# A two-layer decoder trunk on one core: input and output projections cut at the prompt's end instead of in the middle

## The chip, the core and the metric

The kernel runs on one NeuronCore of a Trainium2 chip. The engines named below are TensorE (PE, matrix products, with its weight loads on a row of their own, PEld), VectorE (DVE), ScalarE (ACT), GpSimd (POOL) and SyncE (SP, which issues the transfers). The metric is the device time of one launch in microseconds (us).

## What is computed

The reference is a decoder trunk of two layers, applied to a prompt of 512 tokens and to 8 samples of 8 tokens (64 tokens), with the same weights. Cut to what matters:

```python
def mixer_layer(x, ...states..., norm_w, w_in, ..., w_out):
    h = rmsnorm(x, norm_w)
    proj = jnp.einsum('bld,de->ble', h, w_in)          # 1024 -> 5648 columns
    z, xbc, dt_raw, q, k, v, g_ret, u, g_pool = split_cols(proj, IN_SIZES)
    ...                                                # causal conv, SSD scan -> y_ssd (1024)
    ...                                                # rotary, retention     -> y_ret (512)
    ...                                                # windowed means        -> y_pool (512)
    mix = jnp.concatenate([y_ssd, y_ret, y_pool], axis=-1)
    x = x + jnp.einsum('ble,ed->bld', mix, w_out)      # 2048 -> 1024
    return x, new_states
```

All inputs and outputs are f32. The two `einsum` with `w_in` and `w_out`, over 576 tokens, are the projections this document is about.

## The kernel before

**Layout.** Channels lie on the 128 partitions and the 576 tokens (`TOK`: 512 of the prompt, then 64 of the samples, `SMP`) along the free axis. A projection is cut into units of 128 output channels: unit `u` multiplies a weight block of 8 x 128 x 128 (`KT` = 8 chunks `k` of the contraction) with 576 token columns. A layer has 61 units (`UNITS`): 0 to 44 make the branches' inputs (dt, q, k, v, conv, pool, gates, z), 45 to 52 (`U_OUT` on) are the output projection from `mix`, and 53 to 60 the one from the SSD output in `hin`. Both layers run the same loop body.

**Precision.** Each operand is split into a high part in the type fp32r and a low part, the rest. ACT makes the high part of a weight block (`high`, L799), DVE subtracts it to get the low part (`split`, L1029). `products` (L493 to L500) then makes three matmuls for each `k` and each half of the tokens: high weights x high tokens, high weights x low tokens, low weights x high tokens. A half is 288 columns (`HALF`), and each half has a PSUM bank of its own: `acc_of(u)` is `acc[:, u % 2, :, 0:288]`, two banks for even and two for odd units. So a unit is 2 x 8 x 3 = 48 matmuls of 288 columns. Each matmul has its own weight load in the trace, also where the next one uses the same weights.

**Order.** Each engine runs an order written out by hand, unit by unit ("slots"). PE runs `project(u)`: wait until the weights are split (`w_split`) and until the accumulator of unit u-2 has been read (`evac`, or `x_new` for output units), then the first half over all `k`, then a piece of branch work (`between`), then the second half; after it further branch work may stand (`ssd_turn`, `ssd_y`, `ret_turn`, `pool_mm_`, `ssd_sums`). At the end of a unit PE raises `proj`. ACT then makes the next-but-one weights' high part and reads the accumulator out (`read_out`). DVE's slot `u` runs `before(u)` first, which holds work that PE's `between` of the same unit has made ready (`pool_gate`, `ret_sample_y`, `ret_add`, `ssd_add`), then `split(u + 2)`, which waits for ACT, and then the branch's vector work.

**The stretch of the sample states.** In units 37 to 41 (`S_SST` = 37) the SSD states of the samples (`h0`, eight tiles named h in the trace) are renewed. PE makes four groups of sums (`ssd_sums(q, g)`, L619): (0,0) in the middle of unit 39, (0,1) after unit 39, (1,0) in the middle of unit 40, (1,1) after unit 40. Each but the first waits for DVE to have added the sums before it (`ssd_add`, L1232, semaphore `hs_n`). DVE's order there is: slot 39 begins with `ssd_add(0,0)`, `ssd_decayed` (L1222), `ssd_add(0,1)`; slot 40 begins with `ssd_add(1,0)`, slot 41 with `ssd_add(1,1)`. PE's norm sums after unit 41 wait for the fourth add. `pool_gate(i)` (L1379) reads what `pool_mm_(i)` (L725) has put into the accumulator of unit 33+i, and PE waits for it before it projects unit 35+i into the same banks.

Of the kernel before, what the change touches and what calls it, by code (L numbers as in the profile page):

```python
# [20 lines left out]
HALF = TOK // 2  # L21
KT = D_MODEL // P
# [106 lines left out]
def trunk(nc: bass.Bass, a):  # L129
    with ExitStack() as ctx:  # L130
# [13 lines left out]
        def sem(name):  # L144
# [15 lines left out]
              for i, o in enumerate((2048, 3072, 4096, 5120, 0, 1024, 6144, 8192))]  # L160
# [52 lines left out]
               stk[0:SMP, 0:RP * P], ssq[0:SMP, 0:RP * P]]  # L213
        ones_ = place("ones", [P, P])
# [11 lines left out]
        def acc_of(u):  # L226
            return acc[:, u % 2, :, 0:HALF]

# [27 lines left out]
        evac = sem("acc_read")  # L256
        x_new = sem("x_updated")
# [228 lines left out]
        def _(pe):  # L486
# [6 lines left out]
            def products(u, half, k):  # L493

                out = acc_of(u)[:, half, :]
                hi, lo = operands(u, k, slice(half * HALF, (half + 1) * HALF))
                wh, wl = w_hi[:, u % 2, k, :], w_lo[:, u % 2, k, :]
                pe.matmul(out, wh, hi, start=k == 0, stop=False)  # L498
                pe.matmul(out, wh, lo, start=False, stop=False)  # L499
                return pe.matmul(out, wl, hi, start=False, stop=k == KT - 1)  # L500

            def project_first():

                for step in range(KT + LAG):
                    for u, k in ((0, step), (1, step - LAG)):
# [4 lines left out]
                        for half in range(2):  # L510
                            mm = products(u, half, k)
# [3 lines left out]
            def project(u, between=None):  # L515
# [7 lines left out]
                for half in range(2):  # L523
                    for k in range(KT):
                        if half == 0 and o == 0:
                            pe.wait_ge(mix_lo, k + 1)
                        if half == 0 and o == OUT_CHUNKS:
                            pe.wait_ge(y_lo, k + 1)
                        mm = products(u, half, k)
                    if half == 0 and between is not None:  # L530
                        between()
# [187 lines left out]
            def pool_mm_(g):  # L719

                pe.wait_ge(pooled_ok, g + 1)
                pe.wait_ge(evac, U_GPOOL + g + 1)
                dst = acc_of(U_GPOOL + g)
                for half in range(2):
                    mm = pe.matmul(dst[:, half, :], pw[:, g, :], halves(vT[:, g, :])[:, half, :],  # L725
                                   start=True, stop=True)
                mm.then_inc(pool_mm, 1)
# [64 lines left out]
        def _(eng):  # L792
# [26 lines left out]
            def read_out(u):  # L819

                src = acc_of(u)
                if u == U_DT:
                    go(act(halves(dt_raw), src[0:HEADS], ACT.Identity, bias=hvec[:, 0:1]), evac, u + 1)
                elif u < U_V:
# [4 lines left out]
                    go(act(halves(qk[:, i, :]), src, ACT.Copy, scale=1.0 if i < RP else HD ** -0.5), evac, u + 1)  # L829
                elif u < U_CONV:  # L830
                    go(act(halves(vT[:, u - U_V, :]), src, ACT.Copy), evac, u + 1)
                elif u < U_GRET:
# [4 lines left out]
                    go(act(hb[:, w:w + HALF], src[:, 0, :], ACT.Copy))  # L837
                    go(act(hb[:, w + HALF:w + SEQ], src[:, 1, 0:SEQ - HALF], ACT.Copy))
                    go(act(hb[:, w + SEQ:].rearrange("p (b n) -> p b n", b=NB)[:, :, w:],
                           src[:, 1, SEQ - HALF:].rearrange("p (b n) -> p b n", b=NB), ACT.Copy), evac, u + 1)  # L840
                elif u < U_GPOOL:
                    go(act(halves(qk[:, RP + u - U_GRET, :]), src, ACT.Silu), evac, u + 1)
                elif u < U_Z:
# [3 lines left out]
                    go(act(halves(tmp[:, i % 2, :]), src, ACT.Silu), evac, u + 1)  # L847
                else:
# [5 lines left out]
                    go(act(halves(z_gate[i % 4]), src, ACT.Silu), evac, u + 1)  # L854
# [67 lines left out]
            with eng.Fori(0, DEPTH) as l:  # L922
# [4 lines left out]
                for u in range(UNITS):  # L927
# [21 lines left out]
                    if u < U_OUT:  # L949
                        read_out(u)  # L950
# [13 lines left out]
                    if U_CONV < u <= U_POOL:  # L964
# [770 lines left out]
```

## Time and profile before

| | us |
|---|---|
| median of 3 runs | 1001.88 |
| lowest, highest | 1001.37, 1003.04 |
| the profiled execution | 999.01 |
| its span, first to last instruction | 997.3 |
| PE busy | 946.2 (95%) |
| weight loads busy | 903.7 |
| DVE busy | 675.4 (68%) |
| ACT busy | 436.5 (44%) |

The profiled execution took 999.01 us, of which 1.7 us lie outside its span. A matmul's duration in the trace includes its way through the array, so consecutive matmuls overlap in the timeline: what one matmul costs is read from the distance between the starts of neighbours, not from its duration. A plain f32 matmul stands in the trace as two records, each with a weight load; an fp32r matmul and a transpose stand as one.

### The profile page before, as it was taken

How to read it: one execution, taken by the hardware profiler on the slowest of the kernel's cores; microseconds unless marked ns; L12 is line 12 of the kernel's file. 1: busy time of each engine (PE TensorE's matmuls, PEld its weight loads, DVE VectorE, ACT ScalarE, POOL GpSimd, SP SyncE). 2: the span in 40 equal slices, each digit the busy share in tenths (PEclk: the TensorE clock that was granted, in tenths of full speed). 3: DMA queues.
4: the chain of work that ended last, by engine and by line, in shares of the span. 5: the costliest groups of instructions: out<-in, count | busy, mean ns of one | idle time of the engine just before them, and what ended most of it. 6: DMA issues, size and time to landing. Idle time of an engine off the chain costs nothing.

```text
span 997.3 us, 19050 instructions
## 1 busy us (share of the span) xinstructions
PE 946.2 (95%) x7930; PEld 903.7 (91%) x7930; DVE 675.4 (68%) x912; ACT 436.5 (44%) x707; POOL 44.5 (4%) x148
## 2 busy tenths in 40 slices
PE   1999999999999989999869999999999999999994
PEld 1999999999989779999869999999989987999993
DVE  5796478876895559654459927777679758576444
ACT  5423355334884246522443325532367633644222
POOL 0000011110010000000000001110101000000000
PEclk9999999999999999999979999998999999999997
DMA  6625222234234363322144522221433451552223
GB/s 264 206 71 146 79 64 65 70 100 156 85 103 161 137 231 129 116 85 85 45 156 152 147 86 64 65 64 49 149 107 100 142 199 46 225 184 85 79 55 134
DMA packets 36825, 116.82 MB, mean 117 GB/s; under 512 B 11168, under 2 KB 11808, under 8 KB 35072
## 3 DMA queue, kind: packets, MB, share of 16 engines
q1 hardware_dynamic: 36480, 114.68, 34.6%
q8 instruction: 64, 1.05, 0.4%
q0 software_dynamic: 256, 0.88, 0.3%
q14 instruction: 25, 0.20, 0.1%
HBM read 95.72 MB, written 19.83 MB: 116 GB/s over the span
## 4 chain that ended last, share of the span: by engine, by line
PE 89%; DVE 5%; ACT 2%; DMA 1%; issue 1%; POOLq 0%; DVEq 0%; SPq 0%; ACTq 0%
PE acc L498 26%; PE acc L500 25%; PE acc L499 25%; PE misc L582 2%; DVE h L1232 1%; PE misc L568 1%; PE misc L585 1%; PE misc L635 1%; DVE w_lo L1029 1%; DVE h L1222 1%; PE misc L554 1%; PE misc L676 1%; PE misc L657 1%; PE acc L725 1%; PE misc L599 1%
## 5 line engine op out<-in xcount | busy, mean ns | idle before, releaser
L498 PE MATMUL acc<-hin,w_hi 128*128 128x288 f32 x1696 | 510.3, 301 | 16.8 <-DVE hin L1425 16.7
L499 PE MATMUL acc<-hin,w_hi 128*128 128x288 f32 x1696 | 502.1, 296 | 0.0
L500 PE MATMUL acc<-hin,w_lo 128*128 128x288 f32 x1696 | 502.0, 296 | 0.0
L498 PEld LDWEIGHTS acc<-hin,w_hi 128*128 128x128 f32 x1696 | 320.8, 189 | 31.2 <-DVE hin L1425 18.0
L799 ACT ACTIVATE w_hi<-w_raw 128x1024 fp32r<-128x1024 f32 x122 | 129.1, 1058 | 450.9 <-PE acc L500 439.9
L499 PEld LDWEIGHTS acc<-hin,w_hi 128*128 128x128 f32 x1696 | 321.0, 189 | 0.3
L500 PEld LDWEIGHTS acc<-hin,w_lo 128*128 128x128 f32 x1696 | 320.7, 189 | 0.0
L1029 DVE TENSOR_TENSOR w_lo<-w_raw,w_hi 128x1024 fp32r<-128x1024 f32 x124 | 151.3, 1220 | 197.4 <-ACT w_hi L799 197.3
L498 PE MATMUL acc<-mix,w_hi 128*128 128x288 f32 x256 | 76.2, 298 | 0.0
L500 PE MATMUL acc<-mix,w_lo 128*128 128x288 f32 x256 | 75.5, 295 | 0.0
L499 PE MATMUL acc<-mix,w_hi 128*128 128x288 f32 x256 | 75.4, 294 | 0.0
L1099 DVE SCALAR_TENSOR_TENSOR conv_out<-halo,vec,conv_out 128x600 f32<-128x600 f32 x72 | 60.8, 844 | 2.5
L884 ACT ACTIVATE decay<-decay,token_vecs 128x128 f32<-128x128 f32 (+1 forms) x160 | 47.8, 379 | 1.4
L499 PEld LDWEIGHTS acc<-mix,w_hi 128*128 128x128 f32 x256 | 48.0, 188 | 0.2
L498 PEld LDWEIGHTS acc<-mix,w_hi 128*128 128x128 f32 x256 | 48.0, 188 | 0.2
L500 PEld LDWEIGHTS acc<-mix,w_lo 128*128 128x128 f32 x256 | 48.0, 188 | 0.0
L807 ACT ACTIVATE tmp<-x 128x576 f32<-128x576 f32 x24 | 16.3, 683 | 31.2 <-DVE x L1441 30.1
L582 PE MATMUL misc<-decay,xdt 128*64 128x128 f32 (+1 forms) x320 | 27.3, 266 | 0.0
L1441 DVE TENSOR_TENSOR x<-x,acc 128x576 f32<-128x576 f32 x32 | 24.1, 754 | 3.7 <-PE acc L500 0.2
L582 PEld LDWEIGHTS misc<-decay,xdt 128*64 128x64 f32 (+1 forms) x320 | 19.4, 136 | 6.8 <-issue 6.8
L1146 DVE TENSOR_TENSOR xdt<-misc,token_vecs 128x1024 f32<-128x1024 f32 x10 | 12.2, 1225 | 19.6 <-PE misc L559 19.4
L1158 DVE TENSOR_TENSOR decay<-decay,scores 128x1024 f32<-128x1024 f32 (+1 forms) x20 | 21.5, 1113 | 2.4 <-ACT decay L891 1.7
(204 smaller groups left out, 1017.5 us busy)
## 6 DMA issues: line engine op xcount, KB each, us to landing
w_raw<-in_w SPq DMA_DIRECT2D x124, 512.0 KB, 3.7
decay<-cum_rows SPq DMA_DIRECT2D x8, 1024.0 KB, 6.0
h<-in_ssm SPq DMA_DIRECT2D x16, 512.0 KB, 6.2
out_ssm_s<-h SPq DMA_DIRECT2D x16, 512.0 KB, 6.8
x_kept<-x SPq DMA_DIRECT2D x2, 2304.0 KB, 8.5
x<-x_kept SPq DMA_DIRECT2D x8, 576.0 KB, 5.8
x<-in_x SPq DMA_DIRECT2D x4, 576.0 KB, 5.9
out_y<-x SPq DMA_DIRECT2D x4, 576.0 KB, 2.9
```

The lines of the kernel that those rows point to most:

```text
L498: pe.matmul(out, wh, hi, start=k == 0, stop=False)
L499: pe.matmul(out, wh, lo, start=False, stop=False)
L500: return pe.matmul(out, wl, hi, start=False, stop=k == KT - 1)
L582: mm = pe.matmul(dst[r, :], xdt[0:n, h * HD:(h + 1) * HD], decay[0:n, t % 2, h, 0:n], start=True, stop=not inter)
L799: go(act(w_hi[:, u % 2, :, :], w_raw[:, u % RAW, :, :], ACT.Copy), w_hid, n)
L807: go(act(tmp[:, j % 2, :], x[:, j, :], ACT.Square), sqd, j + 1)
L884: go(act(m, m, ACT.Relu, scale=-1.0, bias=tokv[0:n, t, h:h + 1]))
L1029: go(V.tensor_tensor(w_lo[:, u % 2, :, :], w_raw[:, u % RAW, :, :], w_hi[:, u % 2, :, :].bitcast(F32), ALU.subtract), w_split, n)
L1099: ins = V.scalar_tensor_tensor(out=o, in0=h[:, c:c + CVO], scalar=w[c], in1=o, op0=ALU.mult, op1=ALU.add)
L1146: go(V.tensor_tensor(heads(xdt[:, :]), src, dt_b, ALU.mult))
L1158: ins = V.tensor_tensor(m, m, gm[0:n, g, 0:n].unsqueeze(1).to_broadcast([n, 8, n]), ALU.mult)
L1441: go(V.tensor_tensor(halves(x[:, m, :]), halves(x[:, m, :]), acc_of(u), ALU.add), x_new, o + 1)
```

## The change

The projections are cut at column 512, the prompt's end, and not in the middle. For each `k` there are now five matmuls in place of six: three of 512 columns for the prompt, one of 128 columns in which the samples' high and low parts (64 columns each) stand side by side under the high weights, and one of 64 columns, low weights x high tokens, for the samples. All 1728 columns per `k` are there as before. The low parts' product therefore lands in columns of its own (64 to 127 of the second bank), together with the low weights' product, and has to be added to the first 64: for units up to 44 DVE does it at the start of its slot with a copy out of PSUM and an add in PSUM (`fold`, new semaphore `folded`, for which ACT's `read_out` waits); for the output units DVE adds it to `x` with one more instruction. `k` is now the outer loop and `between` stands after the fourth `k`. ACT reads the accumulator as one row of 576 (the convolution's halo in two pieces, not three). The pool's matmul is cut at 512 too.

```diff
+LEFT = SEQ
...
+        low = xbc_two[:, 10, TOK:]
...
         def acc_of(u):
-            return acc[:, u % 2, :, 0:HALF]
+            return acc[:, u % 2, :, :].rearrange("p a n -> p (a n)")[:, 512 - LEFT:512 - LEFT + TOK]
...
-            def products(u, half, k):
-
-                out = acc_of(u)[:, half, :]
-                hi, lo = operands(u, k, slice(half * HALF, (half + 1) * HALF))
+            def products(u, k):
+                out = acc_of(u)
+                a, b = slice(0, LEFT), slice(LEFT, TOK)
+                m = mix[:, k // 4, :, k % 4, :] if U_OUT <= u < U_OUT + OUT_CHUNKS else hin[:, :, k, :]
                 wh, wl = w_hi[:, u % 2, k, :], w_lo[:, u % 2, k, :]
-                pe.matmul(out, wh, hi, start=k == 0, stop=False)
-                pe.matmul(out, wh, lo, start=False, stop=False)
-                return pe.matmul(out, wl, hi, start=False, stop=k == KT - 1)
+                first, last = k == 0, k == KT - 1
+                both = acc[:, u % 2, 1, 0:2 * SMP].rearrange("p (a n) -> p a n", a=2)
+                pe.matmul(out[:, a], wh, m[:, 0, a], start=first, stop=False)
+                pe.matmul(out[:, a], wh, m[:, 1, a], start=False, stop=False)
+                pe.matmul(both, wh, m[:, :, b], start=first, stop=False)
+                pe.matmul(both[:, 1, :], wl, m[:, 0, b], start=False, stop=last)
+                return pe.matmul(out[:, a], wl, m[:, 0, a], start=False, stop=last)
...
-                for half in range(2):
-                    for k in range(KT):
...
-                        mm = products(u, half, k)
-                    if half == 0 and between is not None:
+                for k in range(KT):
...
+                    mm = products(u, k)
+                    if k == KT // 2 - 1 and between is not None:
                         between()
...
-                for half in range(2):
-                    mm = pe.matmul(dst[:, half, :], pw[:, g, :], halves(vT[:, g, :])[:, half, :],
-                                   start=True, stop=True)
+                for c in (slice(0, LEFT), slice(LEFT, TOK)):
+                    mm = pe.matmul(dst[:, c], pw[:, g, :], vT[:, g, c], start=True, stop=True)
...
-                    go(act(hb[:, w:w + HALF], src[:, 0, :], ACT.Copy))
-                    go(act(hb[:, w + HALF:w + SEQ], src[:, 1, 0:SEQ - HALF], ACT.Copy))
+                    go(act(hb[:, w:w + SEQ], src[:, 0:SEQ], ACT.Copy))
...
                     if u < U_OUT:
+                        wait(folded, u + 1)
                         read_out(u)
...
+            def fold(u):
+
+                wait(proj, u + 1)
+                two = acc[:, u % 2, 1, 0:2 * SMP].rearrange("p (a n) -> p a n", a=2)
+                settle()
+                go(V.tensor_copy(low, two[:, 1, :]))
+                settle()
+                go(V.tensor_tensor(two[:, 0, :], two[:, 0, :], low, ALU.add), folded, u + 1)
...
                 for u in range(UNITS):
+                    if u < U_OUT:
+                        fold(u)
                     before(u)
...
-                        go(V.tensor_tensor(halves(x[:, m, :]), halves(x[:, m, :]), acc_of(u), ALU.add),
+                        go(V.tensor_tensor(x[:, m, :], x[:, m, :], acc_of(u), ALU.add))
+                        settle()
+                        go(V.tensor_tensor(x[:, m, SEQ:], x[:, m, SEQ:], acc[:, u % 2, 1, SMP:2 * SMP], ALU.add),
                            x_new, o + 1)
```

`low` is a column range that no other work uses: the SSD's copy of the samples in chunks 10 and 11 of `xbc_two` is no longer written.

On PE, the middle of unit 39. Before, the last `k` of the first half, the sums, and the first two `k` of the second half:

```order
L498 MATMUL acc<-hin,w_hi 128x288
L499 MATMUL acc<-hin,w_hi 128x288
L500 MATMUL acc<-hin,w_lo 128x288
L619 MATMUL misc<-xdt_to_end,b_tok_seq 128x512 x4
L498 MATMUL acc<-hin,w_hi 128x288
L499 MATMUL acc<-hin,w_hi 128x288
L500 MATMUL acc<-hin,w_lo 128x288
L498 MATMUL acc<-hin,w_hi 128x288
L499 MATMUL acc<-hin,w_hi 128x288
L500 MATMUL acc<-hin,w_lo 128x288
```

After, the fourth `k`, the sums, and the fifth:

```order
L503 MATMUL acc<-hin,w_hi 128x512
L504 MATMUL acc<-hin,w_hi 128x512
L505 MATMUL acc<-hin,w_hi 128x128
L506 MATMUL acc<-hin,w_lo 128x64
L507 MATMUL acc<-hin,w_lo 128x512
L624 MATMUL misc<-xdt_to_end,b_tok_seq 128x512 x4
L503 MATMUL acc<-hin,w_hi 128x512
L504 MATMUL acc<-hin,w_hi 128x512
L505 MATMUL acc<-hin,w_hi 128x128
L506 MATMUL acc<-hin,w_lo 128x64
L507 MATMUL acc<-hin,w_lo 128x512
```

The sums stand at the same place, half-way through the unit; two short matmuls stand between the long ones, and the one with the low weights is followed by another with the same weights.

On DVE, the end of slot 39 and slot 40, h being the sample states. Before:

```order
L1029 TENSOR_TENSOR w_lo<-w_raw,w_hi 128x1024
L1222 TENSOR_TENSOR h_6_65<-h_6_65,exp_last_sample 128x1024
L1222 TENSOR_TENSOR h_7_66<-h_7_66,exp_last_sample 128x1024
L1232 TENSOR_TENSOR h_4_63<-h_4_63,misc 128x512
L1232 TENSOR_TENSOR h_5_64<-h_5_64,misc 128x512
L1232 TENSOR_TENSOR h_6_65<-h_6_65,misc 128x512
L1232 TENSOR_TENSOR h_7_66<-h_7_66,misc 128x512
L1029 TENSOR_TENSOR w_lo<-w_raw,w_hi 128x1024
```

After:

```order
L1037 TENSOR_TENSOR w_lo<-w_raw,w_hi 128x1024
L1239 TENSOR_TENSOR h_6_65<-h_6_65,exp_last_sample 128x1024
L1239 TENSOR_TENSOR h_7_66<-h_7_66,exp_last_sample 128x1024
L1054 COPY xbc<-acc 128x64
L1056 TENSOR_TENSOR acc<-acc,xbc 128x64
L1249 TENSOR_TENSOR h_4_63<-h_4_63,misc 128x512
L1249 TENSOR_TENSOR h_5_64<-h_5_64,misc 128x512
L1249 TENSOR_TENSOR h_6_65<-h_6_65,misc 128x512
L1249 TENSOR_TENSOR h_7_66<-h_7_66,misc 128x512
L1037 TENSOR_TENSOR w_lo<-w_raw,w_hi 128x1024
```

The fold now heads the slot, in front of the state adds for which PE waits, and it waits itself for the end of the unit's projection.

## Rows read from the trace of the kernel before

**Rows 1.** The page: busy us of the engines, and the chain that ended last.

```profile
PE 946.2 (95%) x7930; PEld 903.7 (91%) x7930; DVE 675.4 (68%) x912; ACT 436.5 (44%) x707; POOL 44.5 (4%) x148
...
PE 89%; DVE 5%; ACT 2%; DMA 1%; issue 1%; POOLq 0%; DVEq 0%; SPq 0%; ACTq 0%
PE acc L498 26%; PE acc L500 25%; PE acc L499 25%; PE misc L582 2%; DVE h L1232 1%; PE misc L568 1%; PE misc L585 1%; PE misc L635 1%; DVE w_lo L1029 1%; DVE h L1222 1%; PE misc L554 1%; PE misc L676 1%; PE misc L657 1%; PE acc L725 1%; PE misc L599 1%
```

**Rows 2.** Page, costliest groups: shapes, count | busy us, mean ns | idle before.

```profile
L498 PE MATMUL acc<-hin,w_hi 128*128 128x288 f32 x1696 | 510.3, 301 | 16.8 <-DVE hin L1425 16.7
...
L499 PEld LDWEIGHTS acc<-hin,w_hi 128*128 128x128 f32 x1696 | 321.0, 189 | 0.3
```

**Rows 3.** Timeline of PE, 450 to 458 us: start, duration, engine, line, operands.

```profile
450.06 0.29 PE L498 MATMUL acc<-hin,w_hi 128*128 128x288 f32 x1
450.19 0.30 PE L499 MATMUL acc<-hin,w_hi 128*128 128x288 f32 x1
450.33 0.29 PE L500 MATMUL acc<-hin,w_lo 128*128 128x288 f32 x1
...
457.61 0.29 PE L498 MATMUL acc<-hin,w_hi 128*128 128x288 f32 x1
```

**Rows 4.** Timeline of PE at the start of layer two.

```profile
507.39 0.45 PE L498 MATMUL acc<-hin,w_hi 128*128 128x288 f32 x1
507.63 0.45 PE L499 MATMUL acc<-hin,w_hi 128*128 128x288 f32 x1
```

**Rows 5.** Table of stretches: from:to, length, busy of PE, PEld, DVE, ACT, POOL, clock, DMA.

```profile
504.00:508.00 4.00, 1.49 (x6) 1.49 (x7) 3.85 (x6) 2.05 (x3) 0.00 (x0) 0.50 1.05 378
...
446.00:458.00 12.00, 12.00 (x92) 12.00 (x91) 3.80 (x5) 2.80 (x3) 0.00 (x0) 1.00 0.27 89
```

**Rows 6.** Timeline of PEld where PE had waited for weights.

```profile
521.78 0.19 PEld L498 LDWEIGHTS acc<-hin,w_hi 128*128 128x128 f32 x1 [0.29 <-DVE w_lo L1029]
521.89 0.19 PEld L499 LDWEIGHTS acc<-hin,w_hi 128*128 128x128 f32 x1
522.02 0.19 PEld L500 LDWEIGHTS acc<-hin,w_lo 128*128 128x128 f32 x1
```

**Rows 7.** The chain in order of time: start, length, what, how many.

```profile
114.77 1.09 PE misc L635 x16
...
238.63 1.72 PE misc L568 x4
...
306.42 0.97 PE acc L725 x4
```

**Rows 8.** Timeline of PE, 230 to 233 us, merged.

```profile
231.45 0.61 PE L556 MATMUL misc<-xbc 128*128 128x128 f32 x4
231.89 0.38 PE L559 MATMUL misc<-tab,xbc 128*128 128x128 f32 x2
```

**Rows 9.** Timeline of DVE, units 37 to 41 of layer one.

```profile
324.99 0.82 DVE L1379 SCALAR_TENSOR_TENSOR vT<-acc,vec,tmp 128x576 f32<-128x576 f32 x1 [1.21 <-PE acc L725]
...
343.91 2.48 DVE L1232 TENSOR_TENSOR h<-h,misc 128x512 f32<-128x512 f32 x4 [1.34 <-PE misc L619]
346.52 2.36 DVE L1222 TENSOR_TENSOR h<-h,exp_last_sample 128x1024 f32<-128x1024 f32 x2
...
358.94 2.48 DVE L1232 TENSOR_TENSOR h<-h,misc 128x512 f32<-128x512 f32 x4
...
367.89 1.62 DVE L1401 TENSOR_TENSOR xbc<-xbc,halo 128x576 f32<-128x576 f32 x2
```

**Rows 10.** Timeline of PE at the fourth state sums, layer one.

```profile
357.73 1.14 PE L619 MATMUL misc<-xdt_to_end,b_tok_seq 32*128 32x512 f32 x8 [1.57 <-DVE h L1232]
```

**Rows 11.** Groups by shape on DVE, whole run.

```profile
L1200 DVE SCALAR_TENSOR_TENSOR xbc<-xbc,vec,misc 128x64 f32<-128x64 f32 x16 | 3.2, 272 | 0.0
```

**Rows 12.** Waits: who for whom, us in total, times, longest.

```profile
ACT w_hi L799 <- PE acc L500: 439.9, 112, 11.6
...
PE misc L706 <- ACT rstd L899: 2.0, 2, 1.0
```

More of the change, by code:

```diff
@@ L256, in trunk @@
         evac = sem("acc_read")
+        folded = sem("sample_parts_folded")
         x_new = sem("x_updated")
@@ L522, in project @@
                     pe.wait_ge(x_new, o - 1)
-                for half in range(2):
-                    for k in range(KT):
[L525 to L529, printed above, removed]
-                    if half == 0 and between is not None:
+                for k in range(KT):
+                    if o == 0:
+                        pe.wait_ge(mix_lo, k + 1)
+                    if o == OUT_CHUNKS:
+                        pe.wait_ge(y_lo, k + 1)
+                    mm = products(u, k)
+                    if k == KT // 2 - 1 and between is not None:
                         between()
@@ L822, in read_out @@
                 if u == U_DT:
-                    go(act(halves(dt_raw), src[0:HEADS], ACT.Identity, bias=hvec[:, 0:1]), evac, u + 1)
+                    go(act(dt_raw, src[0:HEADS], ACT.Identity, bias=hvec[:, 0:1]), evac, u + 1)
                 elif u < U_V:
@@ L828, in read_out @@
                         wait(h_lo, KT)
-                    go(act(halves(qk[:, i, :]), src, ACT.Copy, scale=1.0 if i < RP else HD ** -0.5), evac, u + 1)
+                    go(act(qk[:, i, :], src, ACT.Copy, scale=1.0 if i < RP else HD ** -0.5), evac, u + 1)
                 elif u < U_CONV:
-                    go(act(halves(vT[:, u - U_V, :]), src, ACT.Copy), evac, u + 1)
+                    go(act(vT[:, u - U_V, :], src, ACT.Copy), evac, u + 1)
                 elif u < U_GRET:
@@ L846, in read_out @@
                         wait(pool_out, i - 1)
-                    go(act(halves(tmp[:, i % 2, :]), src, ACT.Silu), evac, u + 1)
+                    go(act(tmp[:, i % 2, :], src, ACT.Silu), evac, u + 1)
                 else:
@@ L853, in read_out @@
                         wait(g_z_used, i - 3)
-                    go(act(halves(z_gate[i % 4]), src, ACT.Silu), evac, u + 1)
+                    go(act(z_gate[i % 4], src, ACT.Silu), evac, u + 1)
             def ssd_row_exps(t):
@@ L970, in _ @@
                         sampled = cvt[:, i % 2, 3 + SEQ:HALO].rearrange("p (b n) -> p b n", b=NB)[:, :, 0:NT]
-                        go(act(xbc_two[:, k, SEQ:].rearrange("p (a b n) -> p a b n", a=2, b=NB),
-                               sampled.unsqueeze(1).to_broadcast([P, 2, NB, NT]), ACT.Silu, bias=cb),
-                           xbc_ok, i + 1)
+                        if k < 10:
+                            go(act(xbc_two[:, k, SEQ:].rearrange("p (a b n) -> p a b n", a=2, b=NB),
+                                   sampled.unsqueeze(1).to_broadcast([P, 2, NB, NT]), ACT.Silu, bias=cb),
+                               xbc_ok, i + 1)
+                        else:
+                            go(act(xbc[:, k, SEQ:].rearrange("p (b n) -> p b n", b=NB), sampled, ACT.Silu, bias=cb),
+                               xbc_ok, i + 1)
                     if S_RET <= u < S_RST and (u - S_RET) % 2 == 0:
@@ L1378, in pool_gate @@
                 settle()
-                go(V.scalar_tensor_tensor(out=halves(vT[:, i, :]), in0=acc_of(U_GPOOL + i), scalar=v_(V_PS + i),
-                                          in1=halves(tmp[:, i % 2, :]), op0=ALU.mult, op1=ALU.mult),
+                go(V.scalar_tensor_tensor(out=vT[:, i, :], in0=acc_of(U_GPOOL + i), scalar=v_(V_PS + i),
+                                          in1=tmp[:, i % 2, :], op0=ALU.mult, op1=ALU.mult),
                    pool_out, i + 1)
```

5 lines of the change are left out of this document (2 added, 3 removed).

## The prediction

> **What bounds the kernel now.** I read the page's busy times and its chain first [rows 1]. PE is busy for 95% of the span, 89% of the chain that ended last lies on it, and about 76% on the three lines of `products` alone. DVE is busy for 68%, and ACT spends 440 us waiting for PE to end a unit [rows 12]. So the kernel lasts as long as PE's string of projection matmuls, and a change of that string counts nearly in full. Next comes the question what one of these matmuls costs. The mean of 301 ns in the page [rows 2] is no answer, since neighbours overlap. In the timeline [rows 3] 57 matmuls lie between the starts at 450.06 and 457.61, which is 132.5 ns each, at a granted clock of 1.00 [rows 5], the 2.4 GHz level. There 288 columns need 120 ns, so 12.5 ns are something else. A unit is 48 x 132.5 = 6.4 us, and both layers have 2 x 61 x 8 = 976 steps of `k`, each now 6 x 132.5 = 795 ns.
>
> **What the 12.5 ns are.** Two rows tell. Where the granted clock was 0.50 (1.2 GHz) the spacing was 240 ns [rows 4, 5], exactly 288 columns, with nothing added. And the row of the weight loads [rows 6] shows that a load starts when the matmul before it starts: one load runs ahead, not more. After a wait, with no matmul running, load (521.78) to next load (521.89) is 110 ns; beside a running fp32r matmul it is 130 ns. So I read the spacing as that of the load: 110 ns alone, up to 133 ns beside a stream. Plain f32 records bear out the 110: a record of 128 columns with a full 128 x 128 load stands at (231.89 - 231.45) / 4 = 110 ns [rows 8]. The other reading is a fixed 12.5 ns on each matmul; it costs nearly the same below.
>
> **The projections after the change.** The columns per `k` stay 1728; what changes is what hides the loads. Three matmuls have 512 columns. Plain records of 512 columns stand at 1.72 / 4 = 430 ns [rows 7], at two cycles a column 427 ns, so 3 ns over. At one cycle a column that is 213 + 3 = 217 ns; with a fixed 12.5 ns it would be 226 ns. The two short ones need 53 and 27 ns for their columns, but each must last as long as the load of the matmul behind it: the load for the low weights starts with the 128-column matmul, and the load behind the 64-column one starts with that, though it fetches the same weights again (the same holds before: L499 loads what L498 had, once for each of its 1696 matmuls [rows 2]). That is 110 to 133 ns each. I take the middle, 121.5, since a short stream disturbs the load for only part of it. Sum per `k`: 3 x 217 + 2 x 121.5 = 894 ns, against 795. That is 99 ns x 976 = **96.6 us more**. Bounds: 651 + 220 = 871 ns (+74 us) and 3 x 226 + 266 = 944 ns (+145 us).
>
> **The fold.** Ninety times DVE now copies 128 x 64 out of PSUM and adds it back. The nearest row is 128 x 64 with PSUM as a source, 0.20 us each in a row, 272 ns alone [rows 11]; two that depend on each other make about 0.5 us (0.4 to 0.6). In an ordinary slot this costs nothing: it runs while ACT makes the next high part, for which DVE's `split` waits anyway, and unit and slot both have 6.4 us or more. The order matters more. `fold(u)` waits for the end of unit `u` and now stands in front of `before(u)`, which until now ran in the middle of the unit. I go through the places where PE waits for what `before` does:
> - Slot 37: `pool_gate(3)` began at 324.99 in mid-unit [rows 9]. Now it follows the fold, and PE needs it for unit 38: 0.5 + 0.8 + 0.1 = 1.4 us idle.
> - Slot 39: `ssd_add(0,0)` ran at 343.91, 2.5 us [rows 9]; PE's sums behind unit 39 need it. Now 0.5 + 2.5 + 0.1 = 3.1 us idle.
> - Slot 40: `ssd_add(1,0)` likewise 3.1 us, less the 1.6 us that PE waited for it already [rows 10]: 1.5 us.
> - Slot 41: `ssd_add(1,1)` (358.94) is needed by the norm sums behind unit 41: 3.1 us, of which about 1.1 us comes back, since PE waited there later for ACT, 1.0 us [rows 12], behind DVE's gates at 367.89 [rows 9]. 2.0 us.
>
> The other such places (`ret_add`, `ret_sample_y`, `pool_gate` 0 to 2) have half a unit or a piece of branch work between them and PE's need. Sum 8.0 us a layer, **16 us**; bounds 8 us, if PE finds part of it idle anyway, and 24 us.
>
> **The rest.** The pool's matmul: two records of 288 columns at 0.97 / 4 = 243 ns twice over [rows 7] become two of 430 and two of at least 110, 1.08 in place of 0.97 us, 8 times: **0.9 us**. The output units' additional DVE add is 0.25 us, hidden except at each layer's end; with the short matmuls at the 0.50 clock of a layer's start that makes **2 us** (0 to 4). ACT's merged halo reads save time on an engine that waits 440 us: nothing. The semaphore `folded` holds up ACT's read-out, but only PE's unit u+2 waits for that, a whole unit later: nothing.
>
> **Sum.** 96.6 + 16 + 0.9 + 2 = 115.5 us on the profiled execution's own 999.0 us (span 997.3 and 1.7 around it): 1114.5. The median of the runs lies 2.9 us above that execution: 1117.
>
> **Rivals.**
> A. *Short fp32r matmuls lose their single pass.* No row has one under 288 columns. If they ran like plain f32, the 128-column one would cost two records, 220 ns [rows 8], and the 64-column one 110 to 220. Sum 981 to 1091 ns, +182 to +289 us; I take 1000 ns, +200 us, with the rest 1222. For it: the trace says nothing of such sizes. Against it: type and operands are the same as at 288.
> B. *Loads do not bind, the other side.* If each short matmul costs its columns and 3 ns, 57 + 30, the sum is 651 + 87 = 738 ns, 56 us less, and with the 19 us of fold and rest the time is 965. With fixed 12.5 ns it is 784 ns and 1010. It would take loads that run two ahead. For it: in pairs of row groups with 64 x 128 weights records stand at 1.09 / 16 = 68 ns [rows 7]. Against it: those lie in different rows of the array, ours use all 128, and rows 6 and 8 show 110. The turning point: the change pays from 19 us / 976 = 20 ns less per `k`, so from a short pair below 124 ns, 62 each.
> The Trainium skill ("TensorE: Matmul & The Clock Gate", "Back-to-back issue gap") gives for a lone matmul N / 2.4 + 2.5 ns, by which the five would make 733 ns, case B.
> C. *Long matmuls cost less than their columns*, at the 132.5 ns of rows 3 also with 512: 3 x 132.5 + 2 x 110 = 618 ns, 173 us less, 848 in all. Against it stand the 430 ns of rows 7, which are all columns, and the 240 ns of rows 4.
> The same section of the Trainium skill states 131 ns for pairs of load and matmul at 512 columns and 81 at 128, which would make 555 ns; the trace disagrees with it at 512.
> D. *DVE falls behind.* If the fold's 0.5 us reached PE in all 90 slots, 45 us would come in place of none: 1162. Against it: DVE's 68% would fall to about 64% of the longer span.
>
> **How the numbers follow.** The forecast's own case 0.66, from 1085 to 1178 by its bounds; A 0.15, B 0.11, C 0.02, D 0.06. The likeliest gives 1117. The range takes in D and most of A: 1080 to 1225. Faster by over 0.2% (about what a measurement here can tell from no change) is C and most of B, 0.10; within it 0.01; slower 0.89.
>
> **What would show it.** In the new timeline: 512-column matmuls 217 ns apart (226: the fixed cost); from the 128-column start to the 64-column start and on to the next 110 to 133 ns each; 53 and 27 would be B, 213 and 107 or doubled records A. A unit of about 7.15 us. New waits of PE's L624 sums and of the norm sums for DVE, 3 us long, and of unit 38 for `pool_gate`, four a layer. Folds of 0.5 us, with ACT's wait for PE still in the hundreds of us. It is wrong from the root if the distance between matmuls is not what sets a unit's length.

## The result: 1141.6 us, 14% slower

| | before | after |
|---|---|---|
| median of the runs, us | 1002.0 | 1141.6 |
| lowest to highest | 1001.4 to 1003.0 | 1140.7 to 1143.4 |
| ratio, 95% interval | | 1.140 (1.138 to 1.143) |
| the profiled execution | 999.0 | 1142.0 |
| its span | 997.3 | 1140.3 |

The change costs 140 us where I had forecast 115 (1117 us, range 1080 to 1225). The direction and what bounds the kernel were right; two terms of the sum were too small, the matmuls of 512 columns and the stretch of the state adds. The page of the kernel after, the lines that answer to [rows 1] and [rows 2]:

```profile
PE 1072.0 (94%) x6954; PEld 898.1 (79%) x6954; DVE 723.3 (63%) x1124; ACT 435.5 (38%) x675; POOL 51.0 (4%) x148
...
PE 94%; DVE 3%; ACT 1%; issue 1%; DMA 0%; POOLq 0%; DVEq 0%; ACTq 0%
PE acc L507 27%; PE acc L503 21%; PE acc L504 20%; PE acc L506 7%; PE acc L505 5%; PE misc L587 2%; DVE h L1249 1%; PE misc L573 1%; PE misc L624 1%; PE misc L590 1%; PE misc L640 1%; PE misc L711 1%; PE misc L559 1%; PE misc L662 1%; PE acc L730 1%; PE misc L681 1%
...
L507 PE MATMUL acc<-hin,w_lo 128*128 128x512 f32 x848 | 409.9, 483 | 0.0
L503 PE MATMUL acc<-hin,w_hi 128*128 128x512 f32 x848 | 345.4, 407 | 20.0 <-DVE hin L1442 17.0
...
L506 PE MATMUL acc<-hin,w_lo 128*128 128x64 f32 x848 | 211.0, 249 | 0.0
...
L505 PE MATMUL acc<-hin,w_hi 128*128 128x128 f32 x848 | 188.1, 222 | 0.0
```

PE is as busy as before and more of the chain lies on it (94%). The two short matmuls, L505 and L506, are in the chain with 5% and 7% and have 11% of the columns together, but neither this share nor a duration is their cost: L506, 64 columns, lasts 249 ns in the trace and L505, 128 columns, 222. One record of L506 starts at 520.90 us, while the load of its weights started at 520.85 and takes 0.19 us, so its time is counted from before its weights are there.

The cost is read from the weight loads instead, since a load starts when the matmul before it starts [rows 6]. The timeline of PEld, start and duration in us, in the middle of a unit:

```profile
520.39 0.19 PEld L504 LDWEIGHTS acc<-hin,w_hi 128*128 128x128 f32 x1
520.62 0.19 PEld L505 LDWEIGHTS acc<-hin,w_hi 128*128 128x128 f32 x1
520.85 0.19 PEld L506 LDWEIGHTS acc<-hin,w_lo 128*128 128x128 f32 x1
520.95 0.19 PEld L507 LDWEIGHTS acc<-hin,w_lo 128*128 128x128 f32 x1
521.07 0.19 PEld L503 LDWEIGHTS acc<-hin,w_hi 128*128 128x128 f32 x1
521.30 0.19 PEld L504 LDWEIGHTS acc<-hin,w_hi 128*128 128x128 f32 x1
```

From the start at 520.39 on, the matmuls stand at 0.23, 0.23, 0.10, 0.12 and 0.23 us: three long ones of 231 ns and two short ones of 110 ns, in sum 914 ns per `k` where [rows 3] gave 795. A unit without branch work takes 7.305 us, before 6.36.

The waits of PE behind other engines, with us in total, number and longest. In the kernel before, the lines that answer to the first two waited 3.2 us (L619, for DVE) and 2.0 us (L706, for ACT) in all [rows 10, 12]:

```profile
PE misc L624 <- DVE h L1249: 12.7, 4, 3.2
PE misc L711 <- DVE h L1249: 6.5, 2, 3.3
PE acc L503 <- DVE vT L1396: 3.0, 2, 1.5
```

So the sum of the forecast stands against the two profiled executions like this:

| term, us | forecast | measured |
|---|---|---|
| projections | 96.6 | 0.945 a unit x 122 units = 115.3 |
| units 37 to 42 beyond that | 16 | 13.7 + 13.3 = 27.0 |
| rest | 2.9 | 143.0 - 115.3 - 27.0 = 0.7 |
| sum | 115.5 | 143.0 |

The rest is what is left over and no measurement of the pool's and the output's terms. Unit 23 alone adds 1.6 us to it in one layer and takes 1.4 in the other, by the granted clock, as shown at the end.

The 27 us: units 37 to 42 took 56.2 us in each layer before and 75.6 and 75.2 after (from the start of unit 37 to that of unit 43); 6 x 0.945 = 5.7 of the 19 are the matmuls' own. Of the 27 us, PE's new waits make (12.7 - 3.2) + (6.5 - 2.0) + 3.0 = 17.0. Ten are something else, and the trace shows what. DVE's timeline at the end of unit 40 and PE's sums that wait for it:

```profile
403.90 0.23 DVE L1054 COPY xbc<-acc 128x64 f32<-128x64 f32 x1 [2.90 <-PE acc L507]
404.16 0.23 DVE L1056 TENSOR_TENSOR acc<-acc,xbc 128x64 f32<-128x64 f32 x1
404.49 2.48 DVE L1249 TENSOR_TENSOR h<-h,misc 128x512 f32<-128x512 f32 x4
...
407.03 2.09 PE L624 MATMUL misc<-xdt_to_end,b_tok_seq 32*128 32x512 f32 x8 [3.17 <-DVE h L1249]
```

The table of stretches for the same place (from:to, length, busy time of PE, PEld, DVE, ACT and POOL with counts, granted clock, DMA):

```profile
403.40:407.00 3.60, 0.46 (x4) 0.15 (x2) 2.96 (x7) 3.10 (x5) 0.00 (x0) 1.00 0.00 0
407.00:411.00 4.00, 3.97 (x15) 2.18 (x16) 1.11 (x1) 0.78 (x2) 0.00 (x0) 0.57 0.36 66
411.00:415.00 4.00, 4.00 (x25) 3.45 (x23) 0.00 (x0) 0.00 (x0) 0.00 (x0) 1.00 1.01 402
```

PE has no work from 403.9 to 407.0, and behind that the granted clock is 0.57 in the mean of four microseconds, partly at the 1.2 GHz level. The eight records of L624 last 2.09 us where [rows 10] had 1.14. The same happens behind five of the six waits of 3.2 and 3.3 us (the four microseconds behind them have 0.63, 0.57 and 0.57 in layer one, 0.57 and 0.50 in layer two); behind the last one the clock stays at 1.00, as it does behind the 1.5 us waits for `vT` and behind the waits of 1.6 and 1.0 us in the kernel before.

### The profile page after: what moved, and what is told of

It is laid out like the page before. It is cut to its first block, busy times and chain, and to the rows that moved or that the text cites. A ratio compares the mean times of both kernels' runs of the same rounds, so it can differ in the third digit from the quotient of the medians.

```text
span 1140.3 us, 17412 instructions
## 1 busy us (share of the span) xinstructions
PE 1072.0 (94%) x6954; PEld 898.1 (79%) x6954; DVE 723.3 (63%) x1124; ACT 435.5 (38%) x675; POOL 51.0 (4%) x148
## 4 chain that ended last, share of the span: by engine, by line
PE 94%; DVE 3%; ACT 1%; issue 1%; DMA 0%; POOLq 0%; DVEq 0%; ACTq 0%
PE acc L507 27%; PE acc L503 21%; PE acc L504 20%; PE acc L506 7%; PE acc L505 5%; PE misc L587 2%; DVE h L1249 1%; PE misc L573 1%; PE misc L624 1%; PE misc L590 1%; PE misc L640 1%; PE misc L711 1%; PE misc L559 1%; PE misc L662 1%; PE acc L730 1%; PE misc L681 1%
## 5 line engine op out<-in xcount | busy, mean ns | idle before, releaser
L507 PE MATMUL acc<-hin,w_lo 128*128 128x512 f32 x848 | 409.9, 483 | 0.0
L503 PE MATMUL acc<-hin,w_hi 128*128 128x512 f32 x848 | 345.4, 407 | 20.0 <-DVE hin L1442 17.0
L504 PE MATMUL acc<-hin,w_hi 128*128 128x512 f32 x848 | 334.4, 394 | 0.0
L506 PE MATMUL acc<-hin,w_lo 128*128 128x64 f32 x848 | 211.0, 249 | 0.0
L503 PEld LDWEIGHTS acc<-hin,w_hi 128*128 128x128 f32 x848 | 165.2, 195 | 36.5 <-DVE hin L1442 18.3
L505 PEld LDWEIGHTS acc<-hin,w_hi 128*128 128x128 f32 x848 | 161.5, 190 | 37.9
L504 PEld LDWEIGHTS acc<-hin,w_hi 128*128 128x128 f32 x848 | 162.1, 191 | 34.9
L506 PEld LDWEIGHTS acc<-hin,w_lo 128*128 128x128 f32 x848 | 161.3, 190 | 34.6
L505 PE MATMUL acc<-hin,w_hi 128*128 128x128 f32 x848 | 188.1, 222 | 0.0
L1054 DVE COPY xbc<-acc 128x64 f32<-128x64 f32 x90 | 20.2, 224 | 188.6 <-PE acc L507 186.5
L507 PE MATMUL acc<-mix,w_lo 128*128 128x512 f32 x128 | 61.3, 479 | 0.0
L503 PE MATMUL acc<-mix,w_hi 128*128 128x512 f32 x128 | 51.2, 400 | 0.0
L504 PE MATMUL acc<-mix,w_hi 128*128 128x512 f32 x128 | 49.8, 389 | 0.0
L506 PE MATMUL acc<-mix,w_lo 128*128 128x64 f32 x128 | 31.6, 247 | 0.0
L504 PEld LDWEIGHTS acc<-mix,w_hi 128*128 128x128 f32 x128 | 24.1, 188 | 5.7
L505 PEld LDWEIGHTS acc<-mix,w_hi 128*128 128x128 f32 x128 | 24.0, 188 | 5.6
```

The costliest lines, as they stand in the source:

```text
L503: pe.matmul(out[:, a], wh, m[:, 0, a], start=first, stop=False)
L504: pe.matmul(out[:, a], wh, m[:, 1, a], start=False, stop=False)
L505: pe.matmul(both, wh, m[:, :, b], start=first, stop=False)
L506: pe.matmul(both[:, 1, :], wl, m[:, 0, b], start=False, stop=last)
L507: return pe.matmul(out[:, a], wl, m[:, 0, a], start=False, stop=last)
L1054: go(V.tensor_copy(low, two[:, 1, :]))
```

## The experiments

Twelve kernels test five questions: what the fold costs and why, what a short matmul costs and why, what the loop order does, what the clock does, and whether the idea can pay. Ratios are to the kernel before on the same chip; the ladder (e3) and the two kernels with narrow weights (e7, e9) ran once, for their traces. The kernels that are not joined (e2, e3, e4, e9) leave out the fold and the second add into `x`.

### Fold behind before(u) (e1)

```diff
-                    if u < U_OUT:
-                        fold(u)
                     before(u)
+                    if u < U_OUT:
+                        fold(u)
```

> The changed kernel with one edit: in each DVE slot fold(u) stands behind before(u), not ahead of it. Theory: the fold cost time only through its place, because it made pool_gate(3) and three of the four state adds wait for the end of the unit; beyond the 0.945 us that every unit became longer, units 37 to 42 together became 13.4 us longer per layer, 26.8 us in all. All of it goes: 1141.6 - 27 = 1115 us (1110 to 1120). First rival: only PE's direct idle time goes (16 us as forecast), and the rest has another cause: 1126. Second rival: the place is indifferent and the stretch is slow because units are longer: 1141.

1112.6 us (1111.1 to 1113.1), ratio 1.110 (1.106 to 1.114). That is 29 us less for two lines exchanged. PE's waits for the adds, in the same view as above:

```profile
PE misc L624 <- DVE h L1249: 1.5, 2, 0.8
PE misc L711 <- ACT rstd L902: 1.1, 2, 0.6
```

Units 37 to 42 take 60.6 us, which is 56.2 and the longer matmuls' 5.7 less 1.3. The fold itself, its 90 pairs of instructions, costs nothing here. Both rivals fall.

### Fold alone, on the kernel before (e5)

```diff
+            def fold(u):
+
+                wait(proj, u + 1)
+                part = acc[:, u % 2, 1, 0:SMP]
+                settle()
+                go(V.tensor_copy(low, part))
+                settle()
+                go(V.tensor_tensor(part, part, low, ALU.max), folded, u + 1)
...
+                    if u < U_OUT:
+                        fold(u)
                     before(u)
```

> The kernel before, cut in the middle, plus the fold's two DVE instructions at the head of each slot, here without effect on the result (copy 64 columns, then the maximum of them and their copy), with ACT's read-out waiting for them. It isolates the fold. Theory: the price is the place, units 37 to 42 as in the changed kernel, some 24 to 27 us: 1028 us (1024 to 1030). Rival: the longer units of the changed kernel are needed for it, since here PE already waited 1.6 us for the fourth add: 16 us or less: 1018.

1031.7 us (1031.5 to 1033.7), ratio 1.030 (1.026 to 1.034), a little above the theory's 1024 to 1030. Units 37 to 42 take 72.0 and 70.9 us, 15.8 and 14.7 more than before, so the rival falls. Part of these 15 us is the clock again: the granted clock was 0.50 to 0.65 in the four microseconds behind each of the six waits of 3.2 us. Another part was not foreseen: units 4 to 8 take 6.42 to 6.56 us, unit 7 even 7.33, in place of 6.36. DVE's timeline there:

```profile
62.44 0.22 DVE L1053 COPY xbc<-acc 128x64 f32<-128x64 f32 x1
62.70 0.23 DVE L1055 TENSOR_TENSOR acc<-acc,xbc 128x64 f32<-128x64 f32 x1
62.84 1.22 DVE L1036 TENSOR_TENSOR w_lo<-w_raw,w_hi 128x1024 fp32r<-128x1024 f32 x1
...
68.93 0.22 DVE L1053 COPY xbc<-acc 128x64 f32<-128x64 f32 x1
```

From one fold to the next are 6.49 us without a gap. In these units, where DVE also works on the rotation, its slot is longer than PE's unit of 6.36 us once the fold is in it, and PE waits. In the changed kernel the unit of 7.31 us hides this. An instruction pair of 0.5 us is free only while the slot stays under the unit.

### Filling PE's idle time (e6)

```diff
+            def fill(u):
+
+                pe.wait_ge(evac, u)
+                for i in range(14):
+                    pe.matmul(acc[:, (u + 1) % 2, 0, :], w_hi[:, (u + 1) % 2, i % KT, :], hin[:, 0, i % KT, 0:SEQ],
+                              start=True, stop=True)
...
                         project(u, lambda: ssd_sums(q, 0))
+                        fill(u)
                         ssd_sums(q, 1)
...
+                        fill(u)
                         ret_norm_sum(0)
```

> The changed kernel with 14 matmuls of 512 columns more behind the projections of units 39, 40 and 41, where PE idles 3.2 us for DVE's adds; their product goes into the next unit's accumulator and is overwritten. They take about as long as the wait. Theory: the idle time itself stays, but the granted clock, which fell to the 1.2 GHz level behind these waits (0.57 in the mean of 407 to 411 us and of 420.5 to 424.5 us), does not fall: 5 us a layer less, 1131 us (1128 to 1135). Rival: the clock's fall is not what made units 40 and 41 longer than the 3.1 us of waiting: 1141 or, if the filler lasts longer than the wait, above.

1132.7 us (1131.9 to 1134.2), 8.9 us less than the changed kernel, with 84 matmuls more. The stretches that answer to those above:

```profile
400.00:404.00 4.00, 4.00 (x21) 3.39 (x21) 2.38 (x5) 1.79 (x3) 0.00 (x0) 1.00 0.27 107
404.00:408.00 4.00, 4.00 (x23) 2.46 (x22) 2.42 (x4) 2.10 (x4) 0.00 (x0) 1.00 0.05 11
408.00:412.00 4.00, 4.00 (x24) 3.46 (x23) 0.00 (x0) 0.00 (x0) 0.00 (x0) 1.00 0.80 305
```

The clock stays at 1.00. PE's order and DVE's are the same as in the changed kernel, so the 8.9 us are the price of the clock's fall, most of the 10 us that the waits leave open; units 40 and 41 give it back, 13.3 and 12.6 us where they had 15.1 to 15.6 and 14.6 to 14.9. The rival falls.

### Samples not joined (e2)

```diff
-                pe.matmul(both, wh, m[:, :, b], start=first, stop=False)
-                pe.matmul(both[:, 1, :], wl, m[:, 0, b], start=False, stop=last)
+                pe.matmul(out[:, b], wh, m[:, 0, b], start=first, stop=False)
+                pe.matmul(out[:, b], wh, m[:, 1, b], start=False, stop=False)
+                pe.matmul(out[:, b], wl, m[:, 0, b], start=False, stop=last)
```

> Cut at 512, but the samples' high and low tokens in two matmuls of 64 columns in place of one of 128, so six matmuls per k (512, 512, 64, 64, 64, 512), and no fold at all. Columns per k stay 1728. Theory (a weight load of 110 ns is the floor of each short matmul): per k 3 x 231 + 3 x 110 = 1023 ns against 914 in the changed kernel, +106 us, less the 27 us of the fold's place: 1221 us (1210 to 1230). Rival (short matmuls cost by their columns, and two of 64 columns cost as much as one of 128): 914 ns, 1141.6 - 27 = 1115 us.

1226.0 us (1221.1 to 1236.9), ratio 1.225 (1.216 to 1.234). A unit takes 8.16 us, 1020 ns per `k`: the same columns as in e1 and one matmul more, 107 ns more. Joining was worth that much: the change's two ideas had opposite signs. The cut at 512 alone costs 224 us; joining the parts gives 113 us of it back (1226.0 to 1112.6). The rival, 1115 us, falls.

### A ladder of widths (e3)

```diff
-LEFT = SEQ
+def left_of(u):
+    return 288 + 32 * (u % 8)
...
+                for c in (a, b):
+                    pe.matmul(out[:, c], wh, m[:, 0, c], start=first, stop=False)
+                    pe.matmul(out[:, c], wh, m[:, 1, c], start=False, stop=False)
+                    mm = pe.matmul(out[:, c], wl, m[:, 0, c], start=False, stop=last)
```

> The projections of unit u are cut at column 288 + 32 (u mod 8), so the parts are 288/288, 320/256, 352/224, 384/192, 416/160, 448/128, 480/96 and 512/64, each part three matmuls in a row, no joining and no fold. It measures the spacing of fp32r matmuls at fifteen widths. Theory L (a width costs 6 + 0.44 N ns, with a floor of 110 ns by the weight load): 256: 119, 224: 110, 384: 175, 448: 203, 512: 231, all of 64 to 224: 110. Rival F (the columns at 2.4 GHz and a fixed 12.5 ns, same floor): 384: 172.5, 448: 199, 512: 226, 256: 119. Rival W (at 288 and below the load beside a stream, 132 ns, is the floor, above it the columns and 3 ns): 256 and less: 132, 320: 136, 512: 217.

The loads in a unit cut at 352 and 224:

```profile
98.21 0.19 PEld L507 LDWEIGHTS acc<-hin,w_lo 128*128 128x128 f32 x1
98.32 0.19 PEld L505 LDWEIGHTS acc<-hin,w_hi 128*128 128x128 f32 x1
98.44 0.19 PEld L506 LDWEIGHTS acc<-hin,w_hi 128*128 128x128 f32 x1
98.60 0.19 PEld L507 LDWEIGHTS acc<-hin,w_lo 128*128 128x128 f32 x1
98.76 0.19 PEld L505 LDWEIGHTS acc<-hin,w_hi 128*128 128x128 f32 x1
98.92 0.19 PEld L506 LDWEIGHTS acc<-hin,w_hi 128*128 128x128 f32 x1
```

The matmuls of 224 columns stand at 0.11 us (98.21, 98.32, 98.44), those of 352 at 0.16 (98.44, 98.60, 98.76, 98.92). The mean over all of a width at granted clock 1.00, some 300 to 700 each, in ns:

| columns | 64 to 224 | 256 | 288 | 320 | 352 | 384 | 416 | 448 | 480 | 512 |
|---|---|---|---|---|---|---|---|---|---|---|
| spacing | 110 | 119 | 133 | 147 | 161 | 175 | 190 | 203 | 218 | 231 |
| over the columns at 2.4 GHz | | 12 | 13 | 14 | 14 | 15 | 17 | 16 | 18 | 18 |

Theory L holds at every width to about 1 ns: 6 + 0.44 N ns, and a floor of 110 ns that six widths from 64 to 224 share. Its two figures came from 288 and 512 columns, so the other widths are the test: F is 4 ns short at 416 and 448 and 5 at 480, where L is within 1.5; W misses 256 (119, not 132) and 512 (217). The whole kernel took 1089 us in its one run.

### Narrow weights beside a stream of 288 (e7)

```diff
+                n = {53: 64, 54: 64, 55: 32, 56: 32, 57: 96, 58: 96}.get(u, P)
+                out = out[0:n, :]
-                wh, wl = w_hi[:, u % 2, k, :], w_lo[:, u % 2, k, :]
+                wh, wl = w_hi[:, u % 2, k, 0:n], w_lo[:, u % 2, k, 0:n]
```

> The kernel before, but in six of the last eight units of a layer only some of the 128 output channels are computed (64 in units 53 and 54, 32 in 55 and 56, 96 in 57 and 58; the other channels keep what the accumulator held). The weight loads get shorter, the streams of 288 columns stay. It asks what the 13 ns over the columns' own 120 ns are. Theory (the stream's own cost, 6 + 0.44 N ns, whatever is loaded beside it): all units stay at 132 ns per matmul, 6.36 us. Rival (the load running beside the stream slows it): the 13 ns shrink with the load, to 126 ns with 64 channels and 123 with 32, 6.06 and 5.9 us a unit.

Units 53 to 58 take 6.29, 6.29, 6.26, 6.27, 6.37 and 6.36 us. With a quarter of the load a unit loses 0.1 us of 6.36, 2 ns of a matmul's 13 ns over its columns. The other channels of these units are not computed, here and in e9. So 11 of the 13 ns are not the load's. The theory's 6.36 is missed by 1.5%, the rival's 5.9 by 6%.

### Narrow weights beside a short stream (e9)

```diff
+def left_of(u):
+    return 512
...
+                n = {53: 64, 54: 64, 55: 32, 56: 32, 57: 96, 58: 96}.get(u, P)
```

> Cut at 512 and 64, three matmuls each, not joined, no fold; in units 53 to 58 of each layer only 64, 64, 32, 32, 96, 96 of the 128 output channels are computed, the others keep what the accumulator held. It asks what sets the 110 ns of a short matmul. Theory (its 128-column weight load): with 64 channels the three matmuls of 64 columns stand at 57 ns, with 32 at 30, with 96 at 84; per unit 24 x (0.231 + that) = 6.9, 6.3, 7.6 us against 8.2 with 128. Rival (fp32r matmuls of 64 columns run at four times the columns' time, 107 ns, whatever is loaded): all stay at 110 ns, 8.2 us.

Loads of PEld with 64 of the 128 channels, three matmuls of 64 columns between long ones:

```profile
553.50 0.14 PEld L508 LDWEIGHTS acc<-hin,w_hi 128*64 128x64 f32 x1
553.55 0.14 PEld L509 LDWEIGHTS acc<-hin,w_lo 128*64 128x64 f32 x1
553.61 0.14 PEld L507 LDWEIGHTS acc<-hin,w_hi 128*64 128x64 f32 x1
553.67 0.14 PEld L508 LDWEIGHTS acc<-hin,w_hi 128*64 128x64 f32 x1
553.90 0.13 PEld L509 LDWEIGHTS acc<-hin,w_lo 128*64 128x64 f32 x1
```

and at the border between units with 32 and with 96 channels:

```profile
567.01 0.11 PEld L508 LDWEIGHTS acc<-hin,w_hi 128*32 128x32 f32 x1
567.04 0.11 PEld L509 LDWEIGHTS acc<-hin,w_lo 128*32 128x32 f32 x1
567.07 0.17 PEld L507 LDWEIGHTS acc<-hin,w_hi 128*96 128x96 f32 x1
567.15 0.17 PEld L508 LDWEIGHTS acc<-hin,w_hi 128*96 128x96 f32 x1
567.39 0.16 PEld L509 LDWEIGHTS acc<-hin,w_lo 128*96 128x96 f32 x1
```

The matmuls of 64 columns stand at 56 ns with 64 channels, 32 with 32, 84 with 96 and 110 to 112 with all 128 (mean of each unit's); the units take 6.93, 6.30, 7.60 and 8.21 us, as the theory had it to 0.03 us. The same 64 columns cost whatever their weights take to load. The edit also narrows the matmul's output, but e7 shows that this takes only 2 ns from a stream. The rival falls: there is no slow mode of short fp32r matmuls. The Trainium skill ("TensorE: Matmul & The Clock Gate", "LDWEIGHTS (loading the stationary operand)") gives P / 1.2 ns for the load of P columns of weights, as an estimate 27, 53, 80 and 107 ns for 32 to 128 columns; the runs agree, with 3 to 5 ns on top.

### Loop order, cut in the middle (e4)

```diff
-LEFT = SEQ
+def left_of(u):
+    return 288
```

with the ladder's six matmuls per `k`.

> The changed kernel's order of loops (k outside, the parts inside, branch work after the fourth k, one row read by ACT), but cut in the middle at 288, six matmuls of 288 columns per k, no joining, no fold. Theory: the order of loops costs nothing, a unit is 6.36 us as before: 1002 us (1000 to 1004). Rival: alternating between two PSUM banks within k costs something on each matmul; at 5 ns each that would be 29 us: 1031.

1001.5 us (1000.8 to 1003.2), ratio 1.000 (0.998 to 1.003). The trace has 6.40 us for a unit in place of 6.36, which would be 4.9 us in all. The medians hide it, because the mean granted clock of these runs was higher (median 0.987, the kernel before 0.984) and times go with it by about 1 us for each 0.001. At equal clock, by a straight line fitted to the 23 runs of both kernels, this one is 3.9 us longer (95% interval about 3.0 to 4.8). So the theory that the order costs nothing is off by some 4 us, the rival's 29 us falls, and the order is no cause of the change's 140 us beyond that.

### Joined at a width that hides the loads (e8)

```diff
-LEFT = SEQ
+LEFT = 320
+REST = TOK - LEFT
...
-                both = acc[:, u % 2, 1, 0:2 * SMP].rearrange("p (a n) -> p a n", a=2)
+                both = acc[:, u % 2, 1, 0:2 * REST].rearrange("p (a n) -> p a n", a=2)
```

on e1, with the fold in two pieces of 128 columns.

> The change's idea with widths that hide every load: cut at 320, the other 256 tokens' high and low parts joined in one matmul of 512 columns, so per k 320, 320, 512, 256, 320; the fold (now 256 columns, in two pieces through a buffer of 128) stands behind before(u). By the ladder's spacings, 3 x 148 + 231 + 119 = 794 ns per k against 6 x 133 = 798 (or 795 in the unit's mean), one matmul's fixed part less. Theory: the projections gain 0 to 5 us and the fold is hidden: 998 to 1003 us, no clear difference from the kernel before. Rival: the longer fold (1.1 us, four dependent instructions, ahead of each split) reaches PE in the rotation units and in the SSD stretch: 1010 to 1030 us.

1031.5 us (1029.7 to 1033.5), ratio 1.029 (1.026 to 1.031). A unit without branch work is 6.32 us, 0.04 less than before: the widths 320, 320, 512, 256, 320 hide every load. But the rival is right too:

```profile
PE acc L504 <- DVE w_lo L1038: 14.3, 12, 1.9
...
PE misc L625 <- DVE h L1255: 6.1, 2, 3.1
```

PE waits 14.3 us for `w_lo`, which stands behind the fold, and in units 4 to 8, those with the rotation, a unit takes up to 8.36 us. Now DVE is the bound where its slots were full.

### Joined only where DVE has time (e10, e11, e12)

```diff
+def joined(u):
+    return 9 <= u <= 30 or 34 <= u <= 38 or u >= 45
```

> The joined form with the cut at 320 only in the units in which the all-joined kernel took 6.32 us in place of 6.36 (9 to 30, 34 to 38, 45 to 60, 43 a layer), and six matmuls of 288 columns with no fold in the others, in which the longer fold had reached PE. Theory: 0.04 us x 86 = 3.4 us less than the kernel before, and nothing lost elsewhere: 998.5 us against 1002, ratio 0.9965 (0.993 to 1.000). Rival: the fold still reaches PE in some of these units once their neighbours are different, or the gain is below what can be told: 1002 or more.

1003.1 us (998.6 to 1005.3), ratio 1.001 (0.999 to 1.003). Unit by unit, leaving out unit 23 and the layer's last, 39 of the 41 other joined ones are 0.02 to 0.06 us shorter; unit 47 is 1.0 us longer (norm sums that wait for DVE) and unit 34 by 0.08. Of the not joined ones most are up to 0.04 us longer, by the loop order, and unit 31 by 0.3, since its transposes start that much later.

```diff
-    return 9 <= u <= 30 or 34 <= u <= 38 or u >= 45
+    return 9 <= u <= 29 or 35 <= u <= 38 or u >= 48
...
+                steps = [(k, None) for k in range(KT)] if joined(u) else [(k, h) for h in range(2) for k in range(KT)]
```

> As the kernel before it, with three repairs read from its trace: units that aren't joined keep the old order (first half over all k, then the second), since with k outside a unit of six 288s takes 6.40 and not 6.36 us; units 45 to 47 aren't joined, since unit 47's norm sums waited 1.0 us longer for DVE; nor are 30 and 34. 38 units a layer are joined. Theory: 0.04 us x 76 = 3.0 us less than the kernel before and nothing lost: 999 us against 1002, ratio 0.997 (0.994 to 1.000). Rival: no difference, 1002 us or more, with new waits at other places.

> The same kernel as e11, but the second add into x stands only in the joined output units (in e11 units 45 to 47 did it too, which changes x and costs an instruction). Theory: 0.04 us x 76 = 3.0 us less than the kernel before: 999 us against 1002, ratio 0.997 (0.995 to 0.999). Rival: no difference that can be told, since the waits of unit 23 alone vary by 1.5 to 3 us between executions of one kernel: ratio 0.998 to 1.001 with an interval across 1.

In e11 the units 45 to 47, which are no longer joined, still made the second add into `x`, so that part of the computation is changed there; e12 makes that add in joined units alone.

The results are 1000.4 us (997.1 to 1001.2), ratio 0.9986 (0.9970 to 1.0001), for the first of the two, and 1000.3 us (998.3 to 1003.6), ratio 0.9985 (0.9969 to 1.0001), for the second. In the first one's trace every joined unit but 23 is 0.02 to 0.06 us shorter and nearly all others are unchanged (39 is 0.1 longer). The gain, 1.5 to 2 us, is about half of the 3 that were expected, and the interval touches 1, so by its total time e12 isn't shown to beat the kernel before. What blurs it is the granted clock: at equal clock, by a straight line fitted to all 29 runs, e12 is 1.5 us shorter (95% interval about 1.0 to 2.0). It is the best form found, and a gain of 0.15%.

## Why the forecast was right in kind and short by 25 us

**What bounds the kernel.** Right: PE's string of projection matmuls, and the change counted in full, 115.3 of 143 us.

**Short matmuls.** Right: one load runs ahead and starts with the matmul before it, so each short matmul lasts as long as the load behind it. The size was 110 ns and not the 121.5 that I took as the middle. The 110 ns of [rows 8] were no evidence for it, since a plain record of 128 columns takes 107 + 3 ns for its columns alone, by the rule that I used for [rows 7]; only [rows 6] spoke for it. e9 shows that the load alone sets it, and the ladder that it doesn't grow beside a short stream. The reading of the spacing of 132.5 ns as that of a load slowed by the stream was wrong: e7 takes three quarters of the load away and the spacing falls by 2 ns.

**Long matmuls.** This is the term that failed: 217 ns, measured 231. I took the plain f32 records of 512 columns [rows 7], two cycles a column and 3 ns over, as a guide to one cycle a column. An fp32r stream costs 6 + 0.44 N ns. The fixed 12.5 ns, which I had as the other reading, would have given 226. Three times 14 ns too few and twice 11.5 too many are 19 ns per `k`, 19 us in all; that the second error took back half of the first was luck. (The upper bound of 1178 is 1176 by its own terms.)

**The fold.** Right for the changed kernel: free in ordinary slots, dear by its place, at the four places named; the waits of 3.2 us (forecast 3.1) and 1.5 us (1.4) were there, 17.0 us in all against 16. Missing was the clock: behind the waits of 3.2 us the granted clock fell, behind five of six of them, another 10 us, of which the filler matmuls return 8.9.

**The rivals.** A (a slow mode for short fp32r matmuls) is refuted by e9, B (loads don't bind) and C (512 columns at 132 ns) by the loads' timeline. The rule of the Trainium skill named with C ("TensorE: Matmul & The Clock Gate", "Back-to-back issue gap") has 131 ns at 512 columns and 81 at 128; this kernel shows 231 and 110. D (DVE falls behind) is refuted for the changed kernel by e1, but it is what happened on the shorter units of e5 and e8.

## What to carry to other kernels

Count a split matrix product not by its columns alone but as max(stream, next weight load) for each matmul: with 128 output channels and one load ahead, an fp32r matmul under some 235 columns is paid as 110 ns, so cut evenly, and join short pieces where a cut must be uneven. Put new vector work at the head of a slot only after asking which waits stand behind it: the same two instructions cost 29 us in front of the state adds and nothing behind them. Price a wait of PE with what the clock does after it. And before you compare kernels that differ by less than 1%, look at the mean granted clock of each run.

## What the runs showed of the hardware

- An fp32r stream took 6 + 0.44 N ns for N columns from 256 to 512 at granted clock 1.00, 8 to 12% over N / 2.4 GHz, while [rows 4] at 0.50 shows exactly N / 1.2 GHz. Why the excess grows with N, the runs leave open; only 2 of 13 ns at 288 columns go with the load.
- Weights that stand in the array already are loaded again, at full price: in the changed kernel the load behind the 64-column matmul fetches the same weights and holds it for 111 ns.
- Behind five of six PE waits of 3.2 us the granted clock was at 0.50 to 0.63 in the mean over 4 us, behind waits of 1.5 us it was at 1.00; with the long waits filled by matmuls it stayed at 1.00.
- The clock also fell with PE at work. Unit 23, with its 128 records of 64 x 8 (L676), took 10.5 us in one layer of the kernel before and 13.5 in the other, with the same instructions. The table of stretches:

```profile
192.00:202.49 10.49, 10.49 (x179) 10.31 (x178) 9.38 (x14) 2.10 (x6) 1.31 (x6) 1.00 0.26 66
676.00:689.51 13.51, 13.51 (x180) 13.32 (x177) 9.58 (x14) 2.12 (x6) 1.33 (x6) 0.75 0.18 51
```

PE has no idle time in either, and the granted clock is 1.00 in the first and 0.75 in the second. The unit takes 12.0 us at 0.86 (e5, e8, one layer of e4, e10, e11 and e12). So its steps of 1.5 us, which e12's expectation took for waits, are the clock's.
- The 80 runs of the kernel before that stand beside the experiments last 996 to 1005 us and follow the mean granted clock: 1004.3 us in the mean at 0.980, 998.6 at 0.986. That is why a gain of 3 us is hard to show.
